# A bidirectional DeltaNet and attention encoder: score products in pairs, the output's turn ahead of the second decay product

## The reference, cut to what matters

```python
# DeltaNet, per head: chunked delta rule in both directions, then
o = _rmsnorm_f32(o, norm_w) * jax.nn.silu(z)
y = o.reshape(bsz, seqlen, DN_V_DIM) @ w_out
# attention, per head and block of 128 queries: 128 wide, and 64 wide (rotary)
sc = (jnp.einsum('bhqd,bhkd->bhqk', qn, k_nope)
      + jnp.einsum('bhqd,bkd->bhqk', qr, k_rope)) * scale
p = jax.nn.softmax(sc, axis=-1)
o = jnp.einsum('bhqk,bhkd->bhqd', p, v)
```

## Time and profile before

| | us |
|---|---|
| median of three runs | 1892.78 |
| lowest, highest | 1889.81, 1893.58 |
| profiled execution | 1896.61 |
| its span, first to last instruction | 1894.8 |
| mean granted TensorE clock | 0.918 |

### The profile page before, as it was taken

How to read it: one execution, slowest core, us unless ns; L and a number is a source line. 1 busy time by engine, 2 the same in 40 slices (tenths; PEclk the granted TensorE clock), 3 DMA queues, 4 the chain that set the end, 5 groups by cost and what they waited for, 6 DMA issues and landing times. The chain is left out here.

```text
span 1894.8 us, 20567 instructions
## 1 busy us (share of the span) xinstructions
PE 1610.2 (85%) x6814; PEld 994.5 (52%) x6814; DVE 923.8 (49%) x2045; ACT 325.9 (17%) x737; POOL 118.9 (6%) x101
## 2 busy tenths in 40 slices
PE   7885999999999999999976499946899997489990
PEld 4464576684766758667765144414455453434440
DVE  3662665756766666666555211134245456311115
ACT  2120122121221202212121011101322211011110
POOL 1200200202001020100100100010000000100001
PEclk9997999999999999999986699977899998589995
DMA  5782110101101111100005499942111112669963
GB/s 181 230 261 66 45 44 22 44 22 55 33 22 55 33 33 33 44 0 22 23 1 200 166 301 354 354 141 84 46 45 35 35 34 72 229 190 351 354 233 142
DMA packets 150501, 219.68 MB, mean 116 GB/s; under 512 B 8584, under 2 KB 120448, under 8 KB 150464
## 3 DMA queue, kind: packets, MB, share of 16 engines
q1 hardware_dynamic: 138464, 176.48, 29.2%
q10 hardware_dynamic: 7392, 25.96, 4.0%
q0 software_dynamic: 4608, 16.78, 2.4%
HBM read 175.68 MB, written 43.52 MB: 116 GB/s over the span
## 5 line engine op out<-in xcount | busy, mean ns | idle before, releaser
L1367 PE MATMUL bank<-moe_wgu,moe_xgT 128*96 128x512 f32 x512 | 233.4, 610 | 1.5 <-DVE moe_xgT L1574 1.5
L403 PE MATMUL bank<-xT,wqkv 128*128 128x512 f32 x448 | 211.0, 601 | 9.6 <-DVE conv L873 9.6
L1367 PEld LDWEIGHTS bank<-moe_wgu,moe_xgT 128*96 128x96 f32 x512 | 83.5, 168 | 127.0 <-issue 127.0
L614 PE MATMUL bank<-wo,oT 128*128 128x512 f32 x256 | 128.8, 657 | 7.8 <-ACT oT L764 7.0
L1574 DVE COPY moe_xgT<-bank 128x384 f32<-128x384 f32 x34 | 19.0, 558 | 232.0 <-PE bank L1358 232.0
L486 PE MATMUL bank<-wz,xT 128*128 128x256 f32 x512 | 118.8, 382 | 0.9 <-DVE res L1072 0.9
L403 PEld LDWEIGHTS bank<-xT,wqkv 128*128 128x128 f32 x448 | 78.1, 191 | 74.3 <-issue 63.6
L1384 PE MATMUL bank<-moe_wd,moe_hidT 128*96 128x512 f32 x256 | 115.3, 593 | 1.9 <-DVE moe_hidT L1582 1.9
L486 PEld LDWEIGHTS bank<-wz,xT 128*128 128x128 f32 x512 | 96.6, 192 | 14.3 <-issue 1.7
L797 POOL TENSOR_TENSOR qkd<-dec,kqm 128x512 f32<-128x512 f32 x32 | 47.6, 1519 | 803.2 <-DVE kqm L919 803.2
L873 DVE SCALAR_TENSOR_TENSOR conv<-bank,taps,conv 128x510 f32<-128x510 f32 (+1 forms) x128 | 95.1, 743 | 0.6
(11 more groups left out here) (317 smaller groups left out, 2438.9 us busy)
## 6 DMA issues: line engine op xcount, KB each, us to landing
moe_wgu<-moe_w_gate SPq DMA_DIRECT2D x32, 1024.0 KB, 10.6
moe_wgu<-moe_w_up SPq DMA_DIRECT2D x32, 1024.0 KB, 13.2
moe_wd<-moe_w_down SPq DMA_DIRECT2D x32, 1024.0 KB, 6.5
wqkv<-dn_w_in SPq DMA_DIRECT2D x32, 512.0 KB, 4.0
moe_x_rows<-slots_x ACTq DMA_DIRECT2D x34, 384.0 KB, 7.3
slots_y<-moe_y_rows ACTq DMA_DIRECT2D x32, 384.0 KB, 6.0
slots_x<-o SPq DMA_DIRECT2D x1, 9984.0 KB, 52.6
slots_y<-o SPq DMA_DIRECT2D x1, 9984.0 KB, 93.1
```

The source lines that it names most:

```text
L403: mm = pe.matmul(bank[:], wqkv[:, ct, k], xT[:, k], start=k == 0, stop=k == KD - 1)
L614: mm = pe.matmul(bank[:], oT[:, h, tt], wo[:, h, half * 512:(half + 1) * 512], start=h == 0, stop=h == 1)
L1367: mm = pe.matmul(ps[2][0:CAP], xgT[:, r, k], wgu[:, r, k].rearrange("p a f -> p (a f)"), start=k == 0, stop=k == KD - 1)
```

## The change

Two parts.

In the DeltaNet, `prepare` of TensorE and of ScalarE gets a function to call ahead of the second decay: the turn of the output (`turn_o`) on TensorE and its scaling (`take_o`) on ScalarE. So the order is D0, the turns of conv, the turn of the output, D1, the projection, and on ScalarE D0, squares, v, `oT`, D1. The turn uses banks 0 and 1, those of z and y, in place of 2 and 3. In the last head, which prepares nothing, the order stays. The first `prepare` ahead of the loop calls nothing in between.

In the attention, the four score tiles go in two pairs: both products over 128 rows, then both over 64 rows, which lie on different halves of the partitions and go to different banks.

```diff
--- before.py
+++ after.py
@@ -107,6 +107,7 @@
 
 PROJECT = [("proj0", 0), ("proj1", 1), ("proj2", 0), ("proj3", 1)]
 PREPARE = [("D0", 2), ("tr0", 4), ("tr1", 5), ("tr2", 6), ("tr3", 7), ("D1", 3)]
+TURN_O = [("oT0", 0), ("oT1", 1)]
 PREPARE_LATE = [("kT", 2), ("qT", 3), ("KK", 2), ("KQ", 3)]
 
 
@@ -128,7 +129,7 @@
             names += [(f"w{s}{d}", 2 + d), (f"os{s}{d}", 6 + d)]
     if with_next:
         names += PREPARE
-    names += [("oT0", 2), ("oT1", 3)] + [(f"y{n}", n % 2) for n in range(8)]
+    names += TURN_O + [(f"y{n}", n % 2) for n in range(8)]
     if with_next:
         names += PREPARE_LATE
     return Uses(names)
@@ -437,7 +438,7 @@
                     mm = pe.matmul(ps[b][:], wqkv[:, ct, kk], xT[:, kk], start=kk == 0, stop=kk == KD - 1)
                 mm.then_inc(full[b], 1)
 
-            def prepare(uses, i, n):
+            def prepare(uses, i, n, between):
 
                 def decay(h):
                     bank = begin(uses, f"D{h}", i)
@@ -453,6 +454,7 @@
                     for tt in range(TT):
                         mm = pe.transpose(bank[:, tt * P:(tt + 1) * P], conv[:, ct, tt * P:(tt + 1) * P], ident)
                     done(mm, uses, f"tr{ct}")
+                between()
                 decay(1)
 
             def turn_kq(uses, i, n):
@@ -596,15 +598,19 @@
                             mm = pe.matmul(bank[:, h * P:(h + 1) * P], qkd[:, d * 2 + h, tt], vn[:, d, h], start=True, stop=True)
                         done(mm, uses, f"os{step}{d}")
 
+                def turn_o():
+                    for h in range(2):
+                        pe.wait_ge(og_ready, i + 1)
+                        bank = begin(uses, f"oT{h}", i)
+                        for tt in range(TT):
+                            mm = pe.transpose(bank[:, tt * P:(tt + 1) * P], zs[:, tt, h], ident)
+                        done(mm, uses, f"oT{h}")
+
                 if with_next:
-                    prepare(uses, i, i + 1)
-
-                for h in range(2):
-                    pe.wait_ge(og_ready, i + 1)
-                    bank = begin(uses, f"oT{h}", i)
-                    for tt in range(TT):
-                        mm = pe.transpose(bank[:, tt * P:(tt + 1) * P], zs[:, tt, h], ident)
-                    done(mm, uses, f"oT{h}")
+                    prepare(uses, i, i + 1, turn_o)
+                else:
+                    turn_o()
+
                 pe.wait_ge(o_in, (i + 1) * 16)
                 pe.wait_ge(oT_ready, 1 + i * 2 + 2)
                 for n in range(8):
@@ -620,7 +626,7 @@
 
             pe.wait_ge(taps_ready, 1)
             pe.wait_ge(dve_sums, 1)
-            prepare(FIRST_HEAD, -1, 0)
+            prepare(FIRST_HEAD, -1, 0, lambda: None)
             turn_kq(FIRST_HEAD, -1, 0)
             scores(FIRST_HEAD, -1, 0)
             pe.wait_ge(conv_ready, 4)
@@ -757,11 +764,17 @@
                 square_o(1)
                 if with_next:
                     take_gates(i + 1)
-                    prepare(uses, i, i + 1)
-                for h in range(2):
-                    bank = got(uses, f"oT{h}", i)
-                    act.wait_ge(y_ready, 1 + i * 8)
-                    act.mul(oT[:, h].rearrange("p t n -> p (t n)"), bank[:], nw[:, 0:1]).then_inc(oT_ready, 1)
+
+                def take_o():
+                    for h in range(2):
+                        bank = got(uses, f"oT{h}", i)
+                        act.wait_ge(y_ready, 1 + i * 8)
+                        act.mul(oT[:, h].rearrange("p t n -> p (t n)"), bank[:], nw[:, 0:1]).then_inc(oT_ready, 1)
+
+                if with_next:
+                    prepare(uses, i, i + 1, take_o)
+                else:
+                    take_o()
                 if with_next:
                     prepare_late(uses, i, i + 1)
 
@@ -1913,11 +1926,13 @@
                 begin, done = bank_of(uses, i)
                 pe.wait_ge(kv_ready, 3 * i + 2)
                 pe.wait_ge(qrT_ready, i + 1)
-                for n in range(TT):
-                    bank = begin(f"S{n}")
-                    pe.matmul(bank[:], qnT[:, n * P:(n + 1) * P], knT[:], start=True, stop=False)
-                    half = slice(ROPE * (n % 2), ROPE * (n % 2) + ROPE)
-                    done(pe.matmul(bank[:], qrT[half, n // 2], krT[half], start=False, stop=True), f"S{n}")
+                for pair in ((0, 1), (2, 3)):
+                    banks = [begin(f"S{n}") for n in pair]
+                    for n, bank in zip(pair, banks):
+                        pe.matmul(bank[:], qnT[:, n * P:(n + 1) * P], knT[:], start=True, stop=False)
+                    for n, bank in zip(pair, banks):
+                        half = slice(ROPE * (n % 2), ROPE * (n % 2) + ROPE)
+                        done(pe.matmul(bank[:], qrT[half, n // 2], krT[half], start=False, stop=True), f"S{n}")
                 if uses is not FIRST:
                     pe.wait_ge(wo_in, i * 16)
                     output(begin, done, i)
```

## The result

| | before | after |
|---|---|---|
| median, us | 1893.18 (four runs) | 1874.34 (four runs) |
| lowest, highest | 1889.81, 1895.24 | 1872.76, 1877.26 |
| ratio to before | | 0.9904 (95% interval 0.9884 to 0.9924) |
| profiled execution, its span | 1896.61, 1894.8 | 1872.76, 1871.0 |

The change makes the kernel faster by 18.8 us. The forecast was 1886.2 us in 1878 to 1896: the sign was right, the forecast gain was about a third of the measured one, and the time lies outside the range.

What follows compares the result with a forecast made beforehand. TensorE's stream was taken as the bound in attention and, a few waits aside, in DeltaNet. Attention -13.1 (borders -6.3, overlap -6.8) and DeltaNet +6.5 (D1 +3.3, clock +3.2) gave -6.6: 1886.2 us from median 1892.78, range 1878 to 1896.

Steps and rivals of the forecast that it cites:

- What bounds the kernel: TensorE's instruction stream is the time in attention, and in DeltaNet except for a few waits for VectorE or ScalarE.
- The borders in attention: Score loop: changes between 128-row and 64-row products fall from eight to four a head, 0.197 us each, -6.3 us.
- The overlap: Attention score pairs: the second rotary product runs partly beside the first, three slots in place of four, -6.8 us.
- rival 2: Attention: all of the second rotary product is hidden, -13.7 us, total -13.5, 1879.3 us; chance 0.08.
- D1 behind the turn: DeltaNet: second decay product moved behind the output's turn starts the projection 0.47 us later, +3.3 us in seven heads.
- The clock: DeltaNet, around the turn: more time at 1.2 GHz from one longer idle time, +0.45 us a head, +3.2 us.
- the busier path: Rival in DeltaNet: busier way to the projection removes the 1.2 GHz stretch, -8.7 us there, 1871 us; chance 0.04.
- Banks, ScalarE's order, DMAs: DeltaNet's other edits: new turn banks gain nothing, D1's exponential has over 7 us of cover, no DMA is moved.
- The sum: Whole kernel: attention -13.1 and DeltaNet +6.5 give -6.6 us, 1886.2 us against the median; chance 0.50.
- The range: Whole kernel's time: 1878 to 1896 us, from rival 2's side to that of a slower clock.

Runs made afterwards that it cites:

- e3: Attention part alone against the kernel before, but pairs are tiles 0 and 2, then 1 and 3, on the same partitions; 1890.73 us, ratio 0.9988.
- e10: Kernel before with all four score tiles in one group, rotary products ordered as tiles 0, 2, 1, 3; 1877.19 us, ratio 0.9912 to before.
- e9: Kernel after the change plus three products with overwritten results in the idle time ahead of the turn; 1868.47 us, ratio 0.9869 to the kernel before.
- e7: Kernel before with the attention pairs, and one overwritten product in each of two idle times around the DeltaNet turn; 1865.38 us, ratio 0.9839.
- e1: DeltaNet part of the change alone, attention as in the kernel before; 1896.16 us, ratio 1.0014 to before.
- e4: DeltaNet part alone against the kernel before, with only the second of D1's two products behind the turn; 1888.22 us, ratio 0.9975.
- e6: Kernel before in its old order, plus one overwritten product in each of TensorE's two idle times around the turn; 1882.24 us, ratio 0.9933.
- e5: Attention part alone against the kernel before, with all four score tiles in one group; 1872.10 us, ratio 0.9885.
- e8: Kernel before with four score tiles in one group, and overwritten products in the two idle times around the turn; 1860.14 us, ratio 0.9815.

## Why the prediction was right or wrong

**What bounds the kernel**: right. TensorE's stream was the time in attention, and what it lost the kernel lost: 19.9 us in the trace.

**The borders in attention**: right. I said four borders at 0.197 us a head, 6.3 us in all; e3 shows 0.78 us a head. That a change of the half is free, which no row of before showed, holds in the kernel after: within a pair there is no gap between the loads (four in 0.30 us). With four in one group, where the half changes three times, it holds as well (5.45 us, two borders less than 5.85).

The Trainium skill's rule that a change of the tiling mode drains the engine and a change of the tile does not (TensorEngine Tiling (Array Packing), Key Properties) agrees in both halves with these rows.

**The overlap**: this is the step that failed. I had three slots for a pair, -6.8 us, "if records start in their order and only neighbours on different rows can overlap". It is two slots, -13.6 us, the upper bound, and rival 2, which I had given 0.08. The traces show in its place that records of different halves do not keep to one order: in e10 four products take two lengths (1.92 us) though two on the same half stand behind each other on the list, and tile 1's product ends ahead of tile 2's. I had argued against rival 2 with the order of the records, which no row had shown.

The Trainium skill (TensorE: Matmul & The Clock Gate, Part 3, What overlaps and what doesn't) says that products start and end in program order. For fp32 products on different halves e10 speaks against it, and the measurement decides.

**D1 behind the turn**: the mechanism was right (wait 2.9 in place of 1.26 us, none ahead of the projection), the size too high: 0.47 us at the projection's start forecast, 0.56 measured at full clock, but 0.30 us a head at its end. I had carried the later start to the end of the head undiminished; the first weight load, the wait of y2 and the wait of the next turn each take up some 0.1 us of it (e9 against e7). Seven heads make 2.1 us where I had 3.3.

**The clock**: the term of +3.2 us was too large. The profile of the kernel after has one stretch in six heads and a double one in one head, which is +1.7; with the 2.1 us of length that is the 3.8 us from the first turn to the last. The profile of e1, the same DeltaNet, has a double one too, but none in its first head, so nothing net. The argument behind it (one idle time of 3.1 us is worse than two of together 2.4 to 2.7) was only half of the matter: e4, with 2.0 us in one piece, has stretches in two heads only. What I did not see is that the stretches of before, 1.6 us in each of seven heads, could be had by filling the idle times (e6); I had given their going 0.04, and by the busier path alone.

**Banks, ScalarE's order, DMAs**: at nothing, and nothing of them shows in the kernel after. D1's exponential starts at 314.95 in its second head; the turned k and q, which take its bank over, come from 321.62 on, 6.7 us later.

**The sum**: -13.1 + 6.5 = -6.6 forecast, -19.9 + about 3 in the profiles, -18.8 in the medians. 6.8 us of the miss is the overlap, 3.5 the DeltaNet. The rest, about 2 us, is no larger than the spread of the runs. The two profiled executions differ by more (23.9 us): 4.2 us lie ahead of the first turn, where VectorE's wait for a DMA to `slots_y` ended 2.9 us sooner and the half clock there was shorter, and 2.2 us behind the attention, neither of which the change touches. **The range** was too narrow on the low side, because it ended at rival 2's time with the clock term at my own value and not at its bound.

## What to carry to other kernels

Matrix products over 64 rows belong side by side on both halves of the partitions, with different banks (one bank for both was not tried), and grouped so that 128 and 64 rows change seldom; two of them then cost as much as one, here in fp32. Look also at what reads the banks behind the group: in the first head the larger group met a wait that the pairs did not. When a step fills a hole of TensorE, ask first what the hole that it leaves behind costs, and what the two idle times do to the granted clock: a product whose result is overwritten, laid into an idle time, can be worth more than a change of the order (e6 gained 0.67%, e1 lost 0.14%). When a bound is open and no row speaks for the middle of it, the range has to reach both ends together with the ends of the other terms.

## What the runs showed of the hardware that was not expected

- Where the first attention head has a wait ahead of its q projection, a stretch stands behind it: the profiles of e3, e5, e8 and e10 have both (waits of 1.0 to 1.9 us, stretches of 3.4 to 6.8 us), those of the other eight kernels neither.
- Products on different halves of the rows pass each other: in e10 four fp32 products in the order low, low, high, high took 1.92 us, as in the order low, high, low, high (1.91 us), and the third on the list ended ahead of the second; two on the same half took that long in e3 (1.92 us).
- The half clock around a pair of idle times of 1.3 and 1.0 us costs 1.6 us (116.18 against 114.57 us a head, e6), and it does not come in every head: in the profiled run of e3, whose DeltaNet is that of before, the first three heads ran at 1.00:

```profile
309.00:319.00 10.00, 7.75 (x28) 1.00 0.31 100
...
538.00:548.00 10.00, 7.75 (x25) 0.83 0.32 100
```

  Its loop is 800.4 us long and not 804.7. That is a part of the spread between runs of one kernel, and one reason why the medians of e3 to e5 are good to a few us only. What decides on whether a head gets its stretch is left open here.
